# Two mixing layers and a gated layer on one core: output products in parts at the ends of the layers, conv tiles turned back one item later

## The reference, cut to what matters

```python
proj = jnp.einsum('bld,de->ble', h, w_in[l])
a, g, zc, q, k, v, za, qi, ki, wi = jnp.split(proj, IN_SPLITS, axis=-1)
u = a * sigmoid(g)                       # 31-tap causal depthwise conv, bias
u = silu(layer_norm(conv(u), g, b))
y_conv = u * silu(zc)
y_attn = sparse_attention(q, k, v, qi, ki, wi, topk) * silu(za)
y = jnp.einsum('ble,ed->bld', jnp.concatenate([y_conv, y_attn], axis=-1), w_out[l])
h = layer_norm(ALPHA * h + y, post_ln_g[l], post_ln_b[l])
```

## Time and profile before

| | us |
|---|---|
| median of three runs | 1014.79 |
| lowest and highest run | 1012.3 and 1015.36 |
| the profiled execution | 1014.03 |
| its span, first to last instruction | 1012.2 |
| PE busy | 982.5 |
| DVE busy | 668.4 |
| ACT busy | 559.6 |
| POOL busy | 232.4 |

### The profile page before, as it was taken

How to read it: one execution, slowest core, us unless ns; L and a number is a source line. 1 busy time by engine, 2 the same in 40 slices (tenths; PEclk the granted TensorE clock), 3 DMA queues, 4 the chain that set the end, 5 groups by cost and what they waited for, 6 DMA issues and landing times.

```text
span 1012.2 us, 15815 instructions
## 1 busy us (share of the span) xinstructions
PE 982.5 (97%) x6084; PEld 819.3 (81%) x6084; DVE 668.4 (66%) x1444; ACT 559.6 (55%) x920; POOL 232.4 (23%) x254
## 2 busy tenths in 40 slices
PE   8999999999999999999999999999999999999997
PEld 7888998986677988888878677888888788888886
DVE  4899999988673499999988756638522333333432
ACT  6685891655343568598165424544646566564442
POOL 0110671125212401077111511624101000000001
PEclk9999999999999999999999899999999999999999
DMA  8876885752001577487475300478777536366662
GB/s 299 198 183 169 214 195 135 174 118 85 1 1 66 143 186 175 121 192 183 125 170 122 118 21 1 169 172 199 180 215 198 116 87 162 88 162 129 173 160 83
DMA packets 23962, 143.92 MB, mean 142 GB/s; under 512 B 2880, under 2 KB 3648, under 8 KB 8272
## 3 DMA queue, kind: packets, MB, share of 16 engines
q0 software_dynamic: 8496, 60.36, 32.2%
q1 hardware_dynamic: 15392, 82.55, 23.0%
HBM read 140.81 MB, written 2.10 MB: 141 GB/s over the span
## 4 chain that ended last, share of the span: by engine, by line
PE 80%; DVE 10%; ACT 3%; issue 2%; POOL 2%; DMA 2%; SPq 1%; POOLq 0%; DVEq 0%; ACTq 0%
PE psum_B L1404 20%; PE psum_A L1404 13%; PE psum_B L1438 8%; PE psum_A L1438 8%; PE psum_A L1600 6%; DVE conv_acc L1918 4%; PE psum_C L1480 2%; PE psum_C L1404 2%; PE psum_A L1815 2%; PE psum_B L1815 2%; DMA w_raw<-in_weights 2%; PE psum_B L1544 2%; POOL w_lo L1184 2%; PE psum_B L1802 2%; PE psum_A L1516 2%
## 5 line engine op out<-in xcount | busy, mean ns | idle before, releaser
L1191 POOL DMA_DIRECT2D w_lo<-in_weights x59 | 52.0, 881 | 545.9 <-ACT w_lo L728 493.7
L1918 DVE SCALAR_TENSOR_TENSOR conv_acc<-u,vec,conv_acc 128x528 f32<-128x528 f32 (+1 forms) x240 | 172.4, 756 | 3.2
L1404 PE MATMUL psum_B<-x_hi,w_hi 128*128 128x272 f32 (+3 forms) x456 | 138.1, 337 | 0.5 <-ACT shifted L785 0.3
L1404 PE MATMUL psum_B<-x_hi,w_lo 128*128 128x272 f32 (+3 forms) x456 | 135.4, 331 | 0.0
L1404 PE MATMUL psum_B<-x_lo,w_hi 128*128 128x272 f32 (+3 forms) x456 | 135.3, 331 | 0.0
L727 ACT ACTIVATE w_hi<-w_raw 128x2048 fp32r<-128x2048 f32 (+2 forms) x73 | 113.4, 1553 | 25.8 <-DMA w_raw<-in_weights 25.3
L728 ACT ACTIVATE w_lo<-w_raw 128x2048 fp32r<-128x2048 f32 (+2 forms) x73 | 112.7, 1545 | 0.0
L1404 PE MATMUL psum_A<-x_hi,w_hi 128*128 128x272 f32 (+3 forms) x368 | 100.1, 315 | 0.8 <-DMA w_lo<-in_weights 0.4
L1404 PE MATMUL psum_A<-x_lo,w_hi 128*128 128x272 f32 (+3 forms) x368 | 98.1, 309 | 0.0
L1404 PE MATMUL psum_A<-x_hi,w_lo 128*128 128x272 f32 (+3 forms) x368 | 97.9, 309 | 0.0
L1404 PEld LDWEIGHTS psum_B<-x_hi,w_hi 128*128 128x128 f32 (+1 forms) x456 | 79.0, 187 | 10.0 <-issue 1.7
(11 more groups left out here) (409 smaller groups left out, 2294.9 us busy)
## 6 DMA issues: line engine op xcount, KB each, us to landing
w_raw<-in_weights SPq DMA_DIRECT2D x65, 1024.0 KB, 5.0
w_lo<-in_weights POOLq DMA_DIRECT2D x57, 1024.0 KB, 8.3
x_first<-in_x_t SPq DMA_DIRECT2D x8, 264.0 KB, 6.3
h<-in_x SPq DMA_DIRECT2D x1, 2048.0 KB, 9.8
out<-h SPq DMA_DIRECT2D x4, 512.0 KB, 2.6
w_raw<-in_weights SPq DMA_DIRECT2D x2, 512.0 KB, 7.6
post_ln_g<-in_post_ln_g SPq DMA_DIRECT2D x2, 512.0 KB, 4.6
post_ln_b<-in_post_ln_b SPq DMA_DIRECT2D x2, 512.0 KB, 6.3
```

What stands on the lines that cost most here:

```text
L1191: pool.dma_start(wlo[n % RING][:, 0:width], io["weights"][n, :, 0:width], accum_op=ALU.add) \
L1404: mm = pe.matmul(ps[0:cols, i, o:o + b - a], w[wp][:, kt, at:at + cols], x[xp][:, kt, a:b], start=(kt == 0 and wp + xp == 0), stop=(kt == ...
L1918: got = dve.scalar_tensor_tensor(dst, src, w, dst, ALU.mult, ALU.add)
```

## The change

It does the following.

- OUTPUT_AT: products at slots 17 and 19 go to 18 and 20; the last product of each layer (tile 3, n=1) leaves this table. LAST_OUTPUT_AT places it in two halves of 12 matmuls, and the conv half of tile 4 whole (layer 0) or in two parts of 6 (layer 1). In layer 0 the conv half comes first (36), then the two halves (37, 38, in C); in layer 1 the two halves (28, 29), then the parts (30, 31). Layer 0's norm of tile 3 goes from slot 38 to 39 and behind the loop.
- Conv tiles: back and tanh at i+4, gate at i+5 at the end of the pair on VectorE, rounding at i+6 on ScalarE in a new list "act_middle" behind the exponentials, low part at i+7. The meta copies of the conv part go from 14 to 16. In the pair's norms VectorE does both norms before the conv bias.
- End of layer 0: on VectorE the norm of tile 3 has the gate of tile 4 between its two instructions; both residuals of tile 4 and its norm stand before x_lo of tile 3. TensorE does the attention half n=1 before the turn of rows 3. GpSimd subtracts one half of the second weight block, does the deviation of tile 4, waits for its norm, and subtracts the other half.
- End of layer 1: both row tiles lie in k's memory; the second inputs of tiles 1 and 2 stand before the last gate; ScalarE rounds x of tile 1 before the first weight block.
- Block 2: the first query halves of tiles 0, 1 and 2 stand before the last key-value product and the turn of rows 4 behind the first of them; the second block of the v input joins LO_BY_POOL.

```diff
 OUTPUT_AT = {
-    0: ((17, 0, 0, "A"), (19, 0, 1, "C"), (22, 1, 0, "A"), (25, 1, 1, "B"), (27, 0, 2, "A"), (29, 1, 2, "A"),
-        (34, 0, 3, "A"), (36, 1, 3, "A")),
-    1: ((17, 0, 1, "A"), (19, 0, 2, "B"), (21, 1, 1, "A"), (23, 1, 2, "A"), (26, 0, 3, "A"), (28, 1, 3, "A")),
+    0: ((18, 0, 0, "A"), (20, 0, 1, "C"), (22, 1, 0, "A"), (25, 1, 1, "B"), (27, 0, 2, "A"), (29, 1, 2, "A"),
+        (34, 0, 3, "A")),
+    1: ((18, 0, 1, "A"), (20, 0, 2, "B"), (21, 1, 1, "A"), (23, 1, 2, "A"), (26, 0, 3, "A")),
 }
-META_AT = ((14, "attn"), (14, "conv"))
-POST_AT = {0: ((0, 26), (1, 28), (2, 32), (3, 38)), 1: ((1, 22), (2, 26), (3, 30))}
-OUTPUT_CONV_AT = {0: 38, 1: 30}
+META_AT = ((14, "attn"), (16, "conv"))
+POST_AT = {0: ((0, 26), (1, 28), (2, 32)), 1: ((1, 22), (2, 26), (3, 30))}
+LAST_OUTPUT_AT = {
+    0: ((36, "wo conv", 0, 0, 4), (37, "wo part", 0, 1, 3, "C", 0, 4), (38, "wo part", 1, 1, 3, "C", 0, 4)),
+    1: ((28, "wo part", 0, 1, 3, "A", 0, 4), (29, "wo part", 1, 1, 3, "A", 0, 4), (30, "wo conv", 0, 0, 2),
+        (31, "wo conv", 0, 2, 4)),
+}
-KV_AND_Q = (("kv", 0), ("kv", 1), ("kv", 2), ("q", 0, 0), ("kv", 3), ("q", 1, 0), ("q", 2, 0), ("q", 3, 0),
+KV_AND_Q = (("kv", 0), ("kv", 1), ("kv", 2), ("q", 0, 0), ("q", 1, 0), ("q", 2, 0), ("kv", 3), ("q", 3, 0),
...
-                                      (1, "wo", 0, 1), (1, "wo", 1, 1), (2, "kv", 0), (2, "q", 0))}
+                                      (1, "wo", 0, 1), (1, "wo", 1, 1), (2, "kv", 0), (2, "q", 0), (2, "vin", 1))}
...
-        todo["pe"][i + 3].append(("back", t, buf))
-        todo["act"][i + 3].append(("tanh", t))
-        todo["dve_middle"][i + 4].append(("y", "conv", t))
-        todo["act"][i + 4].append(("hi", "conv", t))
-        todo["pool"][i + 5].append(("lo", "conv", t))
+        todo["pe"][i + 4].append(("back", t, buf))
+        todo["act"][i + 4].append(("tanh", t))
+        todo["dve"][i + 5].append(("y", "conv", t))
+        todo["act_middle"][i + 6].append(("hi", "conv", t))
+        todo["pool"][i + 7].append(("lo", "conv", t))
...
+    todo["dve"][39 if l == 0 else 29].append(("residual", 1, 3))
...
-        hn = [sb("h_normed0", [P, D], at=K_AT + 4 * D), sb("h_normed1", [P, D], at=where[0])]
+        hn = [sb(f"h_normed{i}", [P, D], at=K_AT + 4 * D * i) for i in range(2)]
...
                     if i + 2 < n:
                         exps(l, i + 2)
                         exps(l, i + 3)
+                    for op in rounded[i]:
+                        y_hi(l, *op[1:])
                     gates(i)
                     take_probs_t(l, i + 1)
...
                 y_hi(l, "attn", 4)
+                if l == DEPTH - 1:
+                    x_hi(l, 1)
                 split_hi(after)
...
                 subtract_hi(after)
-                subtract_hi(after + 1)
-                ln_deviation((l, "post", 4), 4, P)
+                if l < DEPTH - 1:
+                    subtract_hi(after + 1, (0,))
+                    ln_deviation((l, "post", 4), 4, P)
+                    pool.wait_ge(normed.sem, normed.at((l, "x", 4)))
+                    subtract_hi(after + 1, (1,))
+                else:
+                    subtract_hi(after + 1)
+                    ln_deviation((l, "post", 4), 4, P)
...
-            split_lo(NUMBER[(2, "vin", 1)])
+            subtract_hi(NUMBER[(2, "vin", 1)])
...
+            def output_part(l, half, n, t, buf, first, last):
+
+                use = (l, "wo", n, t)
+                ps = (bank[buf][:, 1:2, :] if half else claim(use, buf, (1,)))[:, 0, :]
+                mm = output_half(l, n, half, t, ps, range(first, last))
+                if half and last == 4:
+                    mm.then_inc(psum_full.mark(use), 1)
+
-            def output_conv(l, n):
+            def output_conv(l, n, first=0, last=4):
                 buf, at = OUTPUT_BANK[n]
-                ps = claim((l, "wo", n, 4), buf, (at,))[:, 0, :]
-                output_half(l, n, 0, 4, ps).then_inc(psum_full.mark((l, "wo", n, 4, "conv")), 1)
+                ps = (bank[buf][:, at:at + 1, :] if first else claim((l, "wo", n, 4), buf, (at,)))[:, 0, :]
+                mm = output_half(l, n, 0, 4, ps, range(first, last))
+                if last == 4:
+                    mm.then_inc(psum_full.mark((l, "wo", n, 4, "conv")), 1)
...
                 output_attn(l, 0)
                 if l < DEPTH - 1:
                     turn_rows(l, 2)
+                    output_attn(l, 1)
                 turn_rows(l, 3)
-                output_attn(l, 1)
+                if l == DEPTH - 1:
+                    output_attn(l, 1)
...
-                    if t == 2:
-                        turn_rows(1, 4)
                 else:
                     query_half(t, *half)
+                    if (t, *half) == (0, 0):
+                        turn_rows(1, 4)
...
-            def post_norm(l, t):
+            def post_norm(l, t, between=None):
...
                     .then_inc(dve_step.mark((l, "gain", t)), 1)
+                if between:
+                    between()
...
                         normalise(l, i + 2)
+                        normalise(l, i + 3)
                         for op in early[i]:
                             conv_bias(l, op[1])
-                        normalise(l, i + 3)
...
-                y_part(l, "attn", 4)
-
                 if l < DEPTH - 1:
+                    post_norm(l, 3, lambda: y_part(l, "attn", 4))
                     x_lo(l, 0)
                     x_lo(l, 1)
+                    residual(l, 0, 4)
+                    x_lo(l, 2)
+                    residual(l, 1, 4)
+                    aggregate(l, 4)
+                    post_norm(l, 4)
+                    x_lo(l, 3)
                 else:
                     second_input(1)
                     second_input(2)
+                    y_part(l, "attn", 4)
+                    second_input(3)
                     x_lo(l, 1)
-                    second_input(3)
                     x_lo(l, 2)
```

More of the change, by code:

```diff
@@ L303, in attention_extras @@
     n = len(attention_items(l))
-    todo = {engine: [[] for _ in range(n)] for engine in ("pe", "act", "dve_early", "dve_middle", "dve", "pool")}
+    todo = {engine: [[] for _ in range(n)] for engine in ("pe", "act", "act_middle", "dve_early", "dve_middle", "dve", "pool")}
     for gate in GATES_AHEAD[l][len(GATES_AHEAD[l]) // 2:]:
@@ L353, in attention_extras @@
             todo["pool"][i + 1].append(("input", t))
-    todo["pe"][OUTPUT_CONV_AT[l]].append(("wo conv", 0))
+    for i, *op in LAST_OUTPUT_AT[l]:
+        todo["pe"][i].append(tuple(op))
+    if l == 0:
+        todo["dve"][39].append(("aggregate", 3))
+        todo["pool"][39].append(("deviation", "post", 3))
     if l == 0:
@@ L1593, in output_half @@
                     pe.wait_ge(meta_paired.sem, meta_paired.at((l, part)))
-                for kk in range(4):
+                for kk in kks:
                     kt = half * 4 + kk
```

20 lines of the change are left out of this document (9 added, 11 removed).

## The result

| | before | after |
|---|---|---|
| median of seven runs, us | 1014.0 | 1019.69 |
| lowest and highest run | 1012.3 and 1015.36 | 1016.73 and 1021.03 |
| ratio to before, 95% interval | | 1.0052 (1.0041 to 1.0063) |
| the profiled execution | 1014.03 | 1016.73 |
| its span | 1012.2 | 1014.9 |

The account below looks back on a forecast made before the run. TensorE, busy for 97% of the span, was taken as the bound. Gains of 1.51 + 3.10 less 0.6 and 0.3 make 3.7 us, rounded up to 4: median 1010.8 us, range 1005.5 to 1014.8.

Parts of the forecast that it names:

- Layer 0's two waits: End of layer 0: TensorE's waits of 0.82 us at a turn and 0.69 us for tile 4's norm go, gaining 1.51 us.
- all four waits: End of layer 1: TensorE's waits of 0.83, 0.78, 0.52 and 0.97 us go, a stock of 3.10 us.
- one new one: End of layer 1: a new TensorE wait at the first query half, 0 to 2.1 us, taken as 0.6 us.
- The chain: End of layer 1: DMA, ScalarE, GpSimd's four halves (9.56 us alone), then key tile copies, ending at 657.2 to 659.4 us.
- the drain: Each wait that goes gives back some matmul pipeline drain, not priced apart; 3.7 us was rounded up to 4 us.
- the middle is worth nothing: Middle of both layers: later turns, gates, rounding and moved output products gain nothing, because VectorE sets when TensorE proceeds.
- 0.3 us for the clock: Behind the middles' full stretch: longer low clock costs 0 to about 1.7 us per layer, taken as 0.3 us in all.
- the same list of work: Middles: VectorE's work up to the mask of item 18 is unchanged, so the logits of item 20 come no sooner.
- rival C: Middles: VectorE stands for ScalarE's tanh at conv gates, 0 to 2.38 us each; slower, 1019 at 1.4 us each; chance 0.08.
- the v block: Block 2: GpSimd's subtraction has the second v input block ready in time; nothing lost, bound 0 to 1 us.
- Spared short waits, one in their place: Middles: TensorE loses several short waits, then waits in one longer piece at the logits of item 20.
- The pair of second inputs: End of layer 1: inputs of tiles 1 and 2 take 3.52 us against 1.28 us for one alone, delaying the gate up to 0.7 us.

Follow-up runs that it names:

- order of the DMA mended: Ends alone, with GpSimd issuing block 2's accumulating DMA of the first u block ahead of its last query scale: 1008.92 us, ratio 0.9953.
- ends alone: The kernel after with the middle of both layers as before, edits at the layer ends and v rows kept: 1010.45 us, ratio 0.9977.
- outputs 18/20: The kernel after with conv turns, gates, rounding and low parts back at their earlier items, output products still at 18 and 20: 1017.01 us, ratio 1.0020.
- late rounding: The kernel after with conv turn, tanh, gate early and bias between the norms; rounding and low part late, outputs at 18 and 20: 1020.91 us, ratio 1.0060.
- halves: Ends alone, with each layer's two first output products split, conv halves at items 16 and 18, attention halves at 17 and 19: 1006.78 us, ratio 0.9940.
- filled, weights: The kernel after with 12 useless matmuls added at item 17 of each layer, reading a weight block on both sides: 1016.25 us, ratio 1.0033.

## Why the prediction was wrong

**What held.** The ends of the layers. Layer 0's two waits went and nothing came in their place: 1.51 us predicted, 1.35 measured. Layer 1: all four waits of the earlier trace rows went, and one new one came exactly where it was placed, at the first query half behind the copies of the first key tile, 0.45 us against 0.6 predicted. The chain of the kernel after has the terms in which it was worked out:

```profile
647.54 9.51 POOL w_lo L1197 x4
...
660.25 1.15 ACT square L930 x2
661.40 0.16 ACT qk_row L1058
661.56 0.17 ACT v L1059
```

GpSimd's four halves take 9.51 us against 9.56 predicted for halves that don't collide (11.28 in the earlier trace rows). With the order of the DMA mended the end of layer 1 gives 2.52 us (196.15 to 193.63), the predicted 3.10 - 0.6. The kernel with the ends alone has a median of 1010.45 us; the forecast for the whole change was 1010.8. That these two are so near is partly luck: by the means the ends alone gain 2.4 us and not 4, and in its profiled execution the ends give 1.20 + 0.70 us, since 1.71 us go to the weight DMA. No run prices the drain for which the sum was rounded up by 0.3 us. What failed is the sentence that the middle is worth nothing, priced with 0.3 us for the clock: the middles cost 3.21 + 2.71 us in the profiled execution.

**Where it failed: the clock.** The prediction saw that the pair 16/17 keeps only turns, logits and probabilities times v, and charged 0.3 us, with 1.7 us per layer as its bound. In the profiled execution the low clock is 3.4 us longer in each layer. By the prediction's own rate that is 1.7 us each, an estimate of 3.4 of the 5.9 us lost: rate and bound held there, and the charge of 0.3 us did not. Over the runs the moved outputs alone cost 0.43%, 4.3 us (2 to 6 by the intervals). The length of the low clock is not a property of the kernel that one execution shows: the kernel with the DMA's order changed has the same middle as the ends alone, and its execution shows the low level for nearly all of 6.8 us, against 3.4, and a middle 1.67 us longer:

```profile
237.50:244.30 6.80, 6.16 (x17) 3.43 (x18) 5.01 (x13) 2.65 (x5) 3.27 (x4) 0.51 0.19 78
```

The twelve runs of the ends alone spread over 8.7 us with it. Each run's mean granted clock is on record, so the clock's part can be estimated for all runs: an execution of span s at mean clock c loses at most s x (1 - c), namely all of it if TensorE was busy all the time at the lower level.

| | runs | mean, us | mean clock | lost to the clock, at most, us |
|---|---|---|---|---|
| before | 29 | 1013.98 | 0.9932 | 6.8 |
| after | 7 | 1019.27 | 0.9884 | 11.8 |
| ends alone | 12 | 1011.54 | 0.9938 | 6.3 |
| outputs 18/20 | 12 | 1016.18 | 0.9900 | 10.2 |
| late rounding | 6 | 1020.49 | 0.9885 | 11.7 |
| halves | 6 | 1007.49 | 0.9970 | 3.0 |
| filled, weights | 9 | 1017.24 | 0.9943 | 5.8 |

By this estimate up to 4.9 us of the 5.3 us by which the kernel after is slower are clock, up to 3.8 of the 4.6 us of the moved outputs, and 3.3 of the 4.1 us that the halves gain. Of the 4.3 us of the late rounding it is up to 1.6 us. The added matmuls give back up to 6.0 us of clock for 5.5 us of work.

**Where it failed: "the same list of work" on VectorE.** The list was the same, but not its duration. From the wait at 207 us to the mask of item 18 it is 28.43 us before (235.83 - 207.40) and 28.63 us after: right in layer 0. In layer 1 it is 53.26 us (569.39 - 516.13) and 54.51 us, 1.25 us more, and VectorE's timeline says why:

```profile
250.39 0.69 DVE L2129 SCALAR_TENSOR_TENSOR conv_tanh<-conv_tanh,psum_D 128x512 f32<-128x512 f32 x1 [1.56 <-ACT conv_tanh L913]
...
561.97 0.69 DVE L2129 SCALAR_TENSOR_TENSOR conv_tanh<-conv_tanh,psum_D 128x512 f32<-128x512 f32 x1 [1.35 <-ACT conv_tanh L913]
```

That is **rival C**, given 0.08: the gate stands for ScalarE's tanh, about as long as its 1.4 us, but only at one gate of a full stretch. The counter-argument, that the tanh is done within 0.4 us of the gate, was wrong there: ScalarE's copy of probabilities waits for the turn first, and with the half block's rounding behind it (1.05 us) the tanh begins at 561.28, 0.65 us after VectorE was free.

The second cause was in nobody's list, and acts behind that mask. VectorE's instructions in the two middles are the same in number, but they take 130.8 us in the kernel after and 122.8 us before; up to the mask there is no difference (25.12 and 48.29 us before, 25.19 and 48.15 after). It is 123.7 us in the ends alone and 130.1 us with outputs at 18 and 20 and everything else early. So the moved outputs bring nearly all of it, and the late rounding hardly any. In layer 0 the 24 norms of probabilities (L2094) alone take 14.0 us with outputs at 18 and 20, and 10.3 us in the ends alone. It is the contention of the pair shown above: in these two traces all norms that take longer than 0.43 us in layer 0's middle (five, up to 2.31 us, against three, up to 1.03 us), and only these, overlap a subtraction of GpSimd. What this lengthening costs TensorE is not separated from the clock. The prediction used this contention for the v block and not in the middle.

**The new waits.** That L1499 would wait for neg_max in one piece was right (1.36 and 2.39 us). The waits of 1.66 and 1.08 us of probabilities times v for L2121, the attention gate that frees its bank, were missed. They too come with the moved outputs: with outputs at 18 and 20 and the conv gates early they are 1.30 and 0.44 us, and with outputs at 17 and 19 and the gates late there are none. "Spared short waits, one in their place" was thus two in their place.

**The v block.** Nothing lost at the v rows, as predicted, and without the subtraction the wait would have been 5.87 us. The prediction's own figures give 5 (landing at 691 where 686 is wanted); what I expected before that run, 3 us, was too low. The DMA took 10 us and not the median of 8.3. The pair of second inputs of 3.52 us, which the prediction sets against 1.28 us for one, is two instructions, so what the contention had cost there was some 1 us (3.52 - 2 x 1.28). The 0 to 1 us were instead paid at 713 us, 1.09 us, for a DMA queued on GpSimd behind scales that the subtraction had moved back. The step was costed at its own place and not for what stands behind it on the queue.

Left open: by how much the two halves of the change don't add up; how the loss of the middle divides exactly, since waits that fall into low clock cost less and the figures for the clock are upper ones; and what in the light stretch brings the clock down, the kind of work or the short waits in it.

## What to carry to other kernels

When TensorE's dense products are used to fill a stretch of short transposes, where they stand mattered more here than the short waits around them: split them and put the parts between the turns, and read the clock of several executions, not one. A product or step moved for one engine's sake shifts the others too; look at what they run beside in their new place, and at what is queued behind them. Where one engine is full, moving waits about on the others gained nothing here. And a forecast of a few microseconds needs the clock's share of several runs: here it alone was as large as the whole change.

## What the runs showed of the hardware

I had not expected that a kernel could take 5.5 us of useless matmuls and not become slower (1019.69 to 1016.25 us by the medians, 1.0052 to 1.0033 by the ratios). Nor that TensorE falls to its lower level although no wait in the stretch is longer than 2.4 us: in the kernel after it was busy for 15.16 of the 16.60 us up to 236.40, and for 1.32 of the 2.40 us from there to the fall at 238.80, with waits of 1.36 and 0.81 us. The same wait of 1.36 us with 12 dense matmuls behind it brought no fall, and neither did waits of 1.54, 0.74 and 1.30 us in one execution with outputs at 18 and 20. Most of the spread between executions goes with the clock: over twelve runs of the ends alone it falls from 0.997 to 0.989 while the time grows from 1007.48 to 1016.23 us. Of two accumulating DMAs of 1 MB in a row in block 2, the second landed 9.43 to 11.67 us after its issue in the nine executions with 3.65 to 4.26 us between the issues, and after 9.36 us and at most 8.99 us in the two with 5.43 us.
